# A hybrid decoder layer in float32: the gate product as seven block products for eight, and a DMA that adds to the output

## The chip, the cores and the metric

The kernel runs on one core of one Trainium2 chip. The metric is the device time of one execution in microseconds; before the change the median of three runs is 583.5 us (583.44 to 583.79).

## The reference

One decoder layer on 512 tokens of width 1024, in float32: an input projection, block-sparse attention beside a chunked spatial gating, an output projection, a channel MLP with squared ReLU (width 4096), and at the end a gated per-layer embedding. Only the end is changed:

```
h = h + rms_norm(jnp.einsum('bsf,fd->bsd', ff, w_down[i]), mlp_post_g[i])
gate = jax.nn.sigmoid(jnp.einsum('bsd,de->bse', h, w_ple_gate[i]) + b_ple_gate[i])
ple = jnp.einsum('bsp,pd->bsd', p[i], w_ple[i]) * gate
h = h + rms_norm(ple, ple_post_g[i])
```

rms_norm scales each token by one over the root of its mean square and multiplies by a gain row. The gate product is 512x1024 by 1024x1024.

## The kernel before, in words

**Products.** Float32 accuracy comes from splitting each operand into a high part that TensorE takes exactly (the copy to fp32r on ScalarE, "hi") and the remainder (a subtraction on VectorE, "lo"). `product` (line 2337) issues three matmuls for one pair of 128-row blocks: hi by hi, hi by lo, lo by hi. Tokens go in four tiles of 128 (t = 0 to 3), the 1024 output columns in two halves of W = 512. The MLP's up and down products already use a seven-product scheme (`up_product` 2702, `down_product` 2737); their right-hand sums are made partly by VectorE and partly by DMAs on GpSimd's queue that add to what lies in SBUF (`add_x`, line 2139).

**Order of work.** The order on each engine is written out by hand, and each engine goes through its list in order, waiting on semaphores. SyncE's list issues the loads and stores, GpSimd's the accumulating loads.

**The stage around the change.** After the last MLP products come eight tiles of the last part of the down projection (`down_tile`, 2770). For each VectorE adds PSUM to acc (`tail_down`, 1327); per token tile ScalarE squares (`square_down`, 1956), GpSimd takes the power (`rstd`, 2034; two small instructions), and VectorE scales acc and adds it to h (`add_mlp`, 1268; lines 1273 and 1278). TensorE turns h by transposes (`turn_h2`, 2798), ScalarE and VectorE take hi and lo of the turned h straight from PSUM (`h2_turn_lo`, 1281). Meanwhile the gate weights arrive in 8 pairs of 512-column slabs (`gate_pair`, 2251), are copied to hi (`gate_hi`, 1932) and split to lo (`split_lo`, 659, two instructions of 128x512 a pair).

**The gate tiles.** `gate_tile` (2803) makes the tiles of `GATE_TILES` (242), each (token tile, first column, width), nine in all, in the order of the tokens, the last half of token tile 3 in two tiles of 256 columns. A tile is 8 row blocks by three matmuls, 24. After it: VectorE adds the bias from PSUM to acc (`gate_bias`, 1287), ScalarE takes the sigmoid (1964; the last tile straight from PSUM, whose bank was seeded with the bias), VectorE multiplies by ple (`gate_ple`, 1298), ScalarE squares with a sum (`square_ple`, 1974), VectorE multiplies by the gain meanwhile (`gain_ple`, 1307). When the last tile of a token is squared, GpSimd adds the parts and takes the power (lines 2173 to 2194; for the very last tile the root of the sum of the other parts is taken first and squared in as an extra column), and VectorE scales by it and adds to h (`add_ple`, 1316), one instruction per tile. SyncE stores each piece as it is ready (2326).

## Time and profile before

| | |
|---|---|
| median of three runs | 583.5 us |
| span of the profiled execution (first to last instruction) | 581.5 us |
| mean granted TensorE clock, share of full speed | 0.996 |
| TensorE busy | 573.5 us, 99% |
| VectorE busy | 495.2 us, 85% |
| ScalarE busy | 356.4 us, 61% |
| GpSimd busy | 98.6 us, 17% |
| moved by DMA | 89.26 MB, mean 154 GB/s |

The table is read from the top: the profiled execution's own time is its span, 581.5 us, and the runs' median holds 2.0 us more than that span. The busy shares are averages over the whole; the stage that changes begins at about 503 us of the span and is looked at by itself below. In the rows PE is TensorE, PEld its weight load, DVE is VectorE, ACT is ScalarE, POOL is GpSimd and SP is SyncE. Busy times of neighbours can overlap: an instruction's duration is longer than the distance to the next start.

### The profile page before, as it was taken

To read this page: it belongs to the slowest core of one execution; us is meant where nothing else is said; L and a number is where in the kernel's file an instruction comes from. 1 tells how busy PE (TensorE), PEld (TensorE's weight loads), DVE (VectorE), ACT (ScalarE), POOL (GpSimd) and SP (SyncE) were. 2 spreads that over 40 slices of the span, in tenths; PEclk is the share of its full clock that TensorE was granted. 3 is DMA by queue.
4 is the path that set the end of the run, shared out by engine and by line. 5 is a ranking of instruction groups with operands and counts; after the bars stand their busy time and mean duration, and the time that the engine had idled before them with its cause. 6 is when DMAs were issued, how large, how long until landed. Compare 5 with 4: busy or idle time off the path is not lost.

```text
span 581.5 us, 8919 instructions
## 1 busy us (share of the span) xinstructions
PE 573.5 (99%) x3400; PEld 500.8 (86%) x3400; DVE 495.2 (85%) x639; ACT 356.4 (61%) x569; POOL 98.6 (17%) x152
## 2 busy tenths in 40 slices
PE   8999999999999999999999999999999999999995
PEld 7888888888888888989999999999989999988885
DVE  5899986688766998999989999999999899799664
ACT  6896675775646746667656665575655756654422
POOL 0331536000103463001010011010100100011011
PEclk9999999999999999999999999999999999999998
DMA  8982008223003559469485492774753936584011
GB/s 269 345 320 85 0 2 324 76 72 123 25 1 109 202 189 319 87 183 229 96 249 114 119 276 41 215 185 74 264 132 75 285 75 155 207 294 178 0 73 73
DMA packets 26250, 89.26 MB, mean 154 GB/s; under 512 B 3040, under 2 KB 4448, under 8 KB 25696
## 3 DMA queue, kind: packets, MB, share of 16 engines
q1 hardware_dynamic: 20448, 66.59, 32.6%
q0 software_dynamic: 4032, 14.68, 14.3%
q10 hardware_dynamic: 1728, 7.42, 3.4%
q8 instruction: 27, 0.44, 0.3%
q14 instruction: 15, 0.12, 0.1%
HBM read 82.40 MB, written 6.29 MB: 153 GB/s over the span
## 4 chain that ended last, share of the span: by engine, by line
PE 98%; DMA 1%; DVE 0%; ACT 0%; SPq 0%; issue 0%; POOL 0%; DVEq 0%; ACTq 0%
PE psum L2340 31%; PE psum L2344 30%; PE psum L2345 30%; PE psum L2395 2%; PE psum L2578 2%; PE psum L2558 2%; DMA first_raw_a<-weights_dram 1%; PE psum L2409 1%; PE psum L2432 0%; DVE h L1323 0%; ACT w_hi L1393 0%; POOL stat L2192 0%; PE psum L2463 0%; PE psum L2457 0%; PE psum L2437 0%
## 5 line engine op out<-in xcount | busy, mean ns | idle before, releaser
L2340 PE MATMUL psum<-t_hi,a_hi 128*128 128x512 f32 x216 | 84.8, 393 | 0.0
L2344 PE MATMUL psum<-t_lo,a_hi 128*128 128x512 f32 x216 | 84.6, 392 | 0.0
L2345 PE MATMUL psum<-t_hi,a_lo 128*128 128x512 f32 x216 | 84.0, 389 | 0.0
L2340 PE MATMUL psum<-w_hi,actT_hi 128*128 128x512 f32 (+1 forms) x190 | 73.6, 387 | 0.0
L2345 PE MATMUL psum<-w_hi,actT_lo 128*128 128x512 f32 (+1 forms) x190 | 72.4, 381 | 0.0
L2344 PE MATMUL psum<-w_lo,actT_hi 128*128 128x512 f32 (+1 forms) x190 | 72.3, 380 | 0.0
L2345 PE MATMUL psum<-sum_hi,up_lo 128*128 128x256 f32 x224 | 63.4, 283 | 0.0
L2344 PE MATMUL psum<-sum_lo,up_hi 128*128 128x256 f32 x224 | 63.4, 283 | 0.0
L2340 PE MATMUL psum<-sum_hi,up_hi 128*128 128x256 f32 x224 | 63.2, 282 | 0.0
L2345 PE MATMUL psum<-actT_hi,up_lo 128*128 128x256 f32 (+1 forms) x200 | 60.0, 300 | 0.0
L2344 PE MATMUL psum<-actT_lo,up_hi 128*128 128x256 f32 (+1 forms) x200 | 60.0, 300 | 0.0
L2340 PE MATMUL psum<-actT_hi,up_hi 128*128 128x256 f32 (+1 forms) x200 | 59.9, 299 | 0.0
L2142 POOL DMA_DIRECT2D raw_x<-weights_dram x21 | 18.6, 885 | 215.5 <-DVE t_lo L1130 215.1
L1189 DVE TENSOR_TENSOR acc<-acc,psum 128x512 f32<-128x512 f32 x76 | 49.0, 680 | 1.8 <-PE psum L2345 1.8
L985 DVE TENSOR_TENSOR up_lo<-raw,up_hi 128x1024 fp32r<-128x1024 f32 x37 | 46.7, 1262 | 2.6 <-ACT up_hi L1688 2.0
L2345 PEld LDWEIGHTS psum<-t_hi,a_lo 128*128 128x128 f32 x216 | 40.6, 188 | 8.9
L2340 PEld LDWEIGHTS psum<-t_hi,a_hi 128*128 128x128 f32 x216 | 40.7, 189 | 7.1
L2344 PEld LDWEIGHTS psum<-t_lo,a_hi 128*128 128x128 f32 x216 | 40.8, 189 | 6.6
L2344 PEld LDWEIGHTS psum<-sum_lo,up_hi 128*128 128x128 f32 x224 | 42.9, 191 | 1.1
L2340 PEld LDWEIGHTS psum<-sum_hi,up_hi 128*128 128x128 f32 x224 | 42.9, 191 | 1.1
L2345 PEld LDWEIGHTS psum<-sum_hi,up_lo 128*128 128x128 f32 x224 | 42.9, 191 | 0.0
L2345 PEld LDWEIGHTS psum<-w_hi,actT_lo 128*128 128x128 f32 x190 | 35.7, 188 | 6.9
(264 smaller groups left out, 1415.8 us busy)
## 6 DMA issues: line engine op xcount, KB each, us to landing
raw<-weights_dram SPq DMA_DIRECT2D x34, 512.0 KB, 4.5
raw_o<-weights_dram SPq DMA_DIRECT2D x23, 512.0 KB, 4.3
raw_x<-weights_dram POOLq DMA_DIRECT2D x21, 512.0 KB, 5.6
raw_second<-weights_dram SPq DMA_DIRECT2D x14, 512.0 KB, 4.2
raw_x<-weights_dram SPq DMA_DIRECT2D x9, 512.0 KB, 5.9
qk_raw<-weights_dram SPq DMA_DIRECT2D x8, 512.0 KB, 6.8
gate_raw<-weights_dram SPq DMA_DIRECT2D x8, 512.0 KB, 5.1
raw_o<-weights_dram POOLq DMA_DIRECT2D x7, 512.0 KB, 7.1
```

The lines of the kernel that those rows point to most:

```text
L985: nc.vector.tensor_tensor(up_lo[q % UP_SLOTS][:], block_source(step, j), up_hi[q % UP_SLOTS][:].bitcast(F32), ALU.subtract).then_inc(block ...
L1189: nc.vector.tensor_tensor(part, part, bank, how).then_inc(product_added, 1)
L2142: nc.gpsimd.dma_start(raw_x[step % 2][:], weights[down_in_stream(step, rows, half)], accum_op=ALU.add).then_inc(x_added, 16)
L2340: begin = nc.tensor.matmul(out, a_hi, b_hi, start=first, stop=False, skip_group_check=read_between)
L2344: nc.tensor.matmul(out, a_hi, b_lo, start=False, stop=False, skip_group_check=read_between)
L2345: return nc.tensor.matmul(out, a_lo, b_hi, start=False, stop=last, skip_group_check=read_between)
L2395: mm = nc.tensor.transpose(psum[:, banks[name], j * P:(j + 1) * P], source[:, j * P:(j + 1) * P], ident[:])
L2409: mm = nc.tensor.matmul(out, wsT[:, g, :], gv[:, :, g * GD:(g + 1) * GD], start=True, stop=True)
L2558: mm = nc.tensor.transpose(psum[:, bank + s, k * P:(k + 1) * P], probs[:, place_in_group(unit), s, k * P:(k + 1) * P], ident[:])
L2578: mm = nc.tensor.matmul(psum[s * DH:(s + 1) * DH, BANK_O, pair * P:(pair + 1) * P], v[:, k, head * DH:(head + 1) * DH], probsT_of[place_in ...
```

## The change

The gate product is made of seven block products. h has four blocks (token half by row half), the weights have four (row half by column half); the seven products use, on each side, blocks and sums of blocks. In the names below 11, 12, 21 and 22 are blocks, T1 to T4 sums of weight blocks and E, S2, S3 and S4 sums of blocks of h. Each product is made for the two token tiles of a half (j = 0, 1), 4 row blocks by three matmuls, 12 at 512 columns; the last is made in two parts of 256 columns. So there are 14 products, in the order of `GATE_PRODUCTS`.

- Weights: 14 halves of blocks, each 128x1024, are copied to hi by ScalarE and split by VectorE. T1 to T4 come from accumulating loads on GpSimd's queue: T1, T2 and T4 one after another onto the place of block 11, T3 onto a fresh load; each waits until the split of what lies there is done.
- h turned: ScalarE copies it from PSUM to SBUF (`h2_copy_raw`), copies the blocks that are used as they are to hi, and VectorE makes the sums E, S2, S3 and S4 for each j and their lo parts.
- Results: ScalarE seeds the PSUM banks with bias rows (the second is the sum of two, made by GpSimd in SBUF), copies three intermediate results to SBUF (`gate_copy`), and VectorE adds or subtracts (`gate_c11`, `gate_c22`, `gate_fold`). Half of the tiles' sigmoids read PSUM.
- Tiles now finish in the token order 2, 0, 3, 1. For tokens 2 and 0 SyncE stores h into the output early; VectorE then only scales (one scalar_tensor_tensor a tile with the gain row, no separate gain multiply, no add), and an accumulating DMA on GpSimd's queue adds 128x1024 to the output in DRAM.
- The gain row of the MLP, the bias row and the gain row of the embedding are loaded on SyncE's queue in places of their own; a load on ScalarE's queue goes.
- The loads `gate_x` (blocks 21, the base of T3, 22) wait for the split of what lay in their place before. On TensorE each product waits for its weight half, its activation and the bank (PSUM chain 0 and 1, side 2 and 3, E 4 and 5); among them (5, j) waits for `gate_c22(j)` and (6, j) for `gate_fold(j)`.

```diff
+GATE_11, GATE_21, GATE_T1, GATE_T2, GATE_T3, GATE_T4, GATE_22 = range(7)
+GATE_SPLITS = (GATE_11, GATE_T1, GATE_21, GATE_T2, GATE_T3, GATE_T4, GATE_22)
+GATE_SLOT = (1, 2, 0, 3, 1, 2, 0)
+GATE_PRODUCTS = ((0, 0), (1, 0), (0, 1), (1, 1), (2, 0), (3, 0), (2, 1), (4, 0), (3, 1), (5, 0), (4, 1), (6, 0),
+                 (5, 1), (6, 1))
+GATE_CHAIN, GATE_P1, GATE_E = 0, 2, 4
+H2_SPLIT = (0, 1, 2, 3, 5, 7)
+GATE_LAST_PART = GATE_P1 + 1
+OF_E, OF_S2, OF_S3, OF_S4 = range(4)
+GATE_SUMS_SPLIT = ((OF_E, 0), (OF_S2, 0), (OF_E, 1), (OF_S3, 0), (OF_S2, 1), (OF_S3, 1), (OF_S4, 0), (OF_S4, 1))
+GATE_SUMS = ((OF_E, 0), (OF_S2, 0), (OF_S3, 0), (OF_E, 1), (OF_S2, 1), (OF_S3, 1), (OF_S4, 0), (OF_S4, 1))
...
-GATE_TILES = ((0, 0, W), (1, 0, W), (0, W, W), (1, W, W), (2, 0, W), (2, W, W), (3, 0, W),
-              (3, W, W // 2), (3, W + W // 2, W // 2))
-SEEDED = len(GATE_TILES) - 1
+GATE_TILES = ((0, 0, W), (1, 0, W), (2, W, W), (2, 0, W), (3, W, W), (0, W, W), (3, 0, W),
+              (1, W, W // 2), (1, W + W // 2, W // 2))
+TOKENS_DONE = (2, 0, 3, 1)
+ADDED_IN_OUT = (2, 0)
+LAST_GATED = len(GATE_TILES) - 1
...
+            def h2_sum(which, j):
+                a11, a12, a21, a22 = h2_block(0, 0, j), h2_block(0, 1, j), h2_block(1, 0, j), h2_block(1, 1, j)
+                if which == OF_E:
+                    dve.wait_ge(h2_raw, 6 + 2 * j)
+                    first, second, how = a21, a22, ALU.subtract
+                elif which == OF_S2:
+                    dve.wait_ge(x_summed, gate_sum_at(OF_E, j))
+                    first, second, how = gate_e[:, j], a11, ALU.subtract
+                elif which == OF_S3:
+                    first, second, how = a11, a21, ALU.subtract
+                else:
+                    dve.wait_ge(x_summed, gate_sum_at(OF_S2, j))
+                    first, second, how = a12, gate_s2[:, j], ALU.add
+                nc.vector.tensor_tensor(gate_sum_source(which, j), first, second, how).then_inc(x_summed, 1)
...
+            def gate_c11(j):
+                dve.wait_ge(c_copied, gate_copy_at(COPY_C11, j))
+                dve.wait_ge(up_filled, gate_at(1, j))
+                part = acc[:, j, 0:W]
+                nc.vector.tensor_tensor(part, part, psum[:, GATE_P1 + j, :], ALU.add).then_inc(c_summed, 1)
...
+            def gate_fold(j):
+                dve.wait_ge(c_copied, gate_copy_at(COPY_CHAIN, j))
+                if j == 0:
+                    bank = psum[:, GATE_E, :]
+                    nc.vector.tensor_tensor(bank, bank, acc[:, 0, W:2 * W], ALU.subtract).then_inc(gate_folded, 1)
                     return
...
+                if t in ADDED_IN_OUT:
+                    if t == ADDED_IN_OUT[0]:
+                        dve.wait_ge(post_loaded, 48)
+                    dve.wait_ge(pl_rstd, TOKENS_DONE.index(t) + 1)
+                    for i in tiles:
+                        dve.wait_ge(pl_gated, i + 1)
+                        cut = slice(GATE_TILES[i][1], GATE_TILES[i][1] + GATE_TILES[i][2])
+                        nc.vector.scalar_tensor_tensor(out=ple_of(t)[:, cut], in0=acc[:, t, cut],
+                                                       scalar=rstd_pl[:, t:t + 1], in1=ple_gain[:, cut],
+                                                       op0=ALU.mult, op1=ALU.mult).then_inc(out_ready, 1)
+                    return
...
             tail_down(0)
             tail_down(1)
-            splits(SLAB_GATE + 6)
+            gate_split_lo(GATE_T1, 1)
             tail_down(2)
             add_mlp(0)
             tail_down(3)
-            splits(SLAB_GATE + KD)
+            gate_split_lo(GATE_21, 0)
             tail_down(4)
             tail_down(5)
             add_mlp(1)
-            h2_turn_lo(0)
-            h2_turn_lo(1)
-            splits(SLAB_GATE + KD + 2)
+            h2_split_lo(0)
+            h2_split_lo(1)
+            gate_split_lo(GATE_21, 1)
             tail_down(6)
             tail_down(7)
             add_mlp(2)
-            h2_turn_lo(2)
-            h2_turn_lo(3)
+            h2_split_lo(2)
+            h2_split_lo(3)
             add_mlp(3)
-            splits(SLAB_GATE + KD + 4)
-            h2_turn_lo(4)
-            h2_turn_lo(5)
-            splits(SLAB_GATE + KD + 6)
-            h2_turn_lo(6)
-            h2_turn_lo(7)
-            def seed_bias():
-                _, c0, width = GATE_TILES[SEEDED]
-                nc.vector.tensor_copy(psum[:, bank2["gate", SEEDED], 0:width], gate_rows[:, 0, c0:c0 + width]
-                                      ).then_inc(bias_seeded, 1)
-            for i, (t, c0, width) in enumerate(GATE_TILES):
-                gate_bias(i)
-                if i == SEEDED - 6:
-                    dve.wait_ge(*drained["gate", i])
-                    seed_bias()
-                gate_ple(i)
-                if i == gate_tiles_of(t)[-1]:
-                    add_ple(t, *gate_tiles_of(t))
-                else:
-                    gain_ple(i)
+            gate_split_lo(GATE_T2, 0)
+            gate_split_lo(GATE_T2, 1)
+            h2_sum(OF_E, 0)
+            h2_sum(OF_S2, 0)
+            h2_sum_split_lo(OF_E, 0)
+            h2_sum(OF_S3, 0)
+            h2_sum_split_lo(OF_S2, 0)
+            gate_c11(0)
+            gate_split_lo(GATE_T3, 0)
+            gate_split_lo(GATE_T3, 1)
+            h2_split_lo(5)
+            h2_sum(OF_E, 1)
+            h2_sum(OF_S2, 1)
+            h2_sum_split_lo(OF_E, 1)
+            h2_sum_split_lo(OF_S3, 0)
+            h2_sum_split_lo(OF_S2, 1)
+            h2_sum(OF_S3, 1)
+            gate_split_lo(GATE_T4, 0)
+            gate_split_lo(GATE_T4, 1)
+            gate_c11(1)
+            h2_sum(OF_S4, 0)
+            gate_fold(0)
+            gate_c22(0)
+            h2_sum_split_lo(OF_S3, 1)
+            h2_split_lo(7)
+            h2_sum(OF_S4, 1)
+            h2_sum_split_lo(OF_S4, 0)
+            gate_split_lo(GATE_22, 0)
+            gate_split_lo(GATE_22, 1)
+            gate_ple(0)
+            h2_sum_split_lo(OF_S4, 1)
+            gate_fold(1)
+            gate_ple(1)
+            gate_ple(2)
+            gate_ple(3)
+            gate_c22(1)
+            add_ple(2)
+            gain_ple(1)
+            gate_ple(4)
+            gain_ple(4)
+            gate_ple(5)
+            add_ple(0)
+            gate_ple(6)
+            add_ple(3)
+            gate_ple(7)
+            gain_ple(7)
+            gate_ple(8)
+            add_ple(1)
...
+            def h2_copy_raw(i):
+                t, k_half = divmod(i, 2)
+                if i == 0:
+                    act.wait_ge(a_lo_done, FIRST_LAST + 4)
+                act.wait_ge(filled, filled2["h2T", i])
+                nc.scalar.activation(h2_block(t // 2, k_half, t % 2), h2_turned(i), ACT.Copy).then_inc(h2_raw, 1)
+                drained["h2T", i] = (h2_raw, i + 1)
...
+                if (t < 2) == (c0 == 0):
+                    act.wait_ge(c_summed, gate_result_at(t // 2, j))
+                    nc.scalar.activation(z, z, ACT.Sigmoid).then_inc(sig_done, 1)
+                else:
+                    act.wait_ge(up_filled, gate_at(5 if c0 == 0 else 6, j) + (i == LAST_GATED))
+                    nc.scalar.activation(z, gate_result(i), ACT.Sigmoid).then_inc(sig_done, 1)
...
+            gate_split_hi(GATE_T1, 1)
             square_down(0)
-            gate_hi(4)
+            gate_split_hi(GATE_21, 0)
             square_down(1)
-            gate_hi(5)
-            h2_turn_hi(0)
-            h2_turn_hi(1)
+            gate_split_hi(GATE_21, 1)
+            seed_chain(0)
+            seed_chain(1)
+            for i in (0, 1):
+                h2_copy_raw(i)
+                h2_split_hi(i)
             square_down(2)
-            act.wait_ge(filled, filled2["down", 7])
-            act.dma_start(gate_rows[:], rows["gate"]).then_inc(gate_rows_loaded, 16)
-            h2_turn_hi(2)
-            h2_turn_hi(3)
+            for i in (2, 3):
+                h2_copy_raw(i)
+                h2_split_hi(i)
             square_down(3)
-            gate_hi(6)
-            h2_turn_hi(4)
-            h2_turn_hi(5)
-            gate_hi(7)
-            h2_turn_hi(6)
-            h2_turn_hi(7)
-            for i in range(len(GATE_TILES)):
+            gate_split_hi(GATE_T2, 0)
+            gate_split_hi(GATE_T2, 1)
+            seed_e(0)
+            seed_e(1)
+            gate_copy(COPY_C11, 0)
+            h2_copy_raw(4)
+            h2_copy_raw(5)
+            h2_split_hi(5)
+            h2_sum_split_hi(OF_E, 0)
+            h2_sum_split_hi(OF_S2, 0)
+            gate_copy(COPY_C11, 1)
+            gate_split_hi(GATE_T3, 0)
+            gate_split_hi(GATE_T3, 1)
+            h2_copy_raw(6)
+            h2_copy_raw(7)
+            h2_split_hi(7)
+            h2_sum_split_hi(OF_E, 1)
+            h2_sum_split_hi(OF_S3, 0)
+            h2_sum_split_hi(OF_S2, 1)
+            gate_copy(COPY_E, 0)
+            gate_copy(COPY_CHAIN, 0)
+            gate_split_hi(GATE_T4, 0)
+            gate_split_hi(GATE_T4, 1)
+            h2_sum_split_hi(OF_S3, 1)
+            gate_copy(COPY_E, 1)
+            sigmoid(0)
+            h2_sum_split_hi(OF_S4, 0)
+            gate_split_hi(GATE_22, 0)
+            gate_split_hi(GATE_22, 1)
+            h2_sum_split_hi(OF_S4, 1)
+            gate_copy(COPY_CHAIN, 1)
+            sigmoid(1)
+            square_ple(0)
+            sigmoid(2)
+            square_ple(1)
+            sigmoid(3)
+            square_ple(2)
+            square_ple(3)
+            for i in range(4, len(GATE_TILES)):
...
+            def add_gate(block, part):
+                pair = {GATE_T1: 4, GATE_T2: 6, GATE_T4: 2, GATE_T3: 6}[block] + part
+                if block == GATE_T3:
+                    pool.wait_ge(gate_x_loaded[part], first_load + 32)
+                else:
+                    before = {GATE_T1: GATE_11, GATE_T2: GATE_T1, GATE_T4: GATE_T2}[block]
+                    pool.wait_ge(block_lo, gate_split_at(before, part))
+                added = gate_x_added if block == GATE_T3 else gate_y_added[part]
+                nc.gpsimd.dma_start(gate_source(block, part), weights[gate_in_stream(pair)], accum_op=ALU.add
+                                    ).then_inc(added, 16)
...
+            add_gate(GATE_T1, 0)
+            add_gate(GATE_T1, 1)
+            pool.wait_ge(bias_loaded, 16)
+            nc.gpsimd.tensor_tensor(gate_bias_row[:, W:2 * W], gate_bias_row[:, 0:W], gate_bias_row[:, W:2 * W],
+                                    ALU.add).then_inc(bias_summed, 1)
+            add_gate(GATE_T2, 0)
+            down_rstd(0)
+            add_gate(GATE_T2, 1)
+            down_rstd(1)
+            down_rstd(2)
+            add_gate(GATE_T3, 0)
+            down_rstd(3)
+            add_gate(GATE_T3, 1)
+            add_gate(GATE_T4, 0)
+            add_gate(GATE_T4, 1)
...
+                if t in ADDED_IN_OUT:
+                    pool.wait_ge(stored, 16 * len(ADDED_IN_OUT))
+                    pool.wait_ge(out_ready, 2 * (n + 1))
+                    nc.gpsimd.dma_start(out[t * P:(t + 1) * P], ple_of(t), accum_op=ALU.add).then_inc(added_in_out, 16)
...
+            for t in ADDED_IN_OUT:
+                sp.wait_ge(h2_ready, t + 1)
+                sp.dma_start(out[t * P:(t + 1) * P], h[:, t, :]).then_inc(stored, 16)
...
+                for k in range(4):
+                    mm = product(out, x_high[:, k, :], x_low[:, k, :], w_high[:, k, columns], w_low[:, k, columns],
+                                 i == 1 and k == 0, k == 3, read_between=True)
+                mm.then_inc(up_filled, 1)
...
             down_tile(7)
             turn_h2(2)
             turn_h2(3)
-            gate_tile(0)
+            gate_product(0, 0)
+            gate_product(1, 0)
             turn_h2(4)
             turn_h2(5)
-            gate_tile(1)
+            gate_product(0, 1)
+            gate_product(1, 1)
             turn_h2(6)
             turn_h2(7)
-            for i in range(2, len(GATE_TILES)):
-                gate_tile(i)
+            for i, j in GATE_PRODUCTS[4:-1]:
+                gate_product(i, j)
+            gate_product(6, 1, 0)
+            gate_product(6, 1, 1)
```

## Rows read from the trace of the kernel before

**Rows 1.** The page: busy time (us, share, instructions); by engine, the chain that ended last.

```profile
PE 573.5 (99%) x3400; PEld 500.8 (86%) x3400; DVE 495.2 (85%) x639; ACT 356.4 (61%) x569; POOL 98.6 (17%) x152
...
PE 98%; DMA 1%; DVE 0%; ACT 0%; SPq 0%; issue 0%; POOL 0%; DVEq 0%; ACTq 0%
```

**Rows 2.** Timeline of PE in the gate stage: start us, duration us, engine, line, operation, tiles.

```profile
545.00 0.39 PE L2340 MATMUL psum<-w_hi,actT_hi 128*128 128x512 f32 x1
...
569.48 0.28 PE L2340 MATMUL psum<-w_hi,actT_hi 128*128 128x256 f32 x1
...
575.12 0.28 PE L2345 MATMUL psum<-w_hi,actT_lo 128*128 128x256 f32 x1
```

**Rows 3.** Timeline of DVE in the tail of the last tokens; in brackets idle before, releaser.

```profile
565.63 0.69 DVE L1305 TENSOR_TENSOR acc<-acc,ple_late_b 128x512 f32<-128x512 f32 x1 [0.70 <-ACT acc L1972]
...
568.20 1.41 DVE L1323 SCALAR_TENSOR_TENSOR h<-ple_late_b,stat,h 128x512 f32<-128x512 f32 x2 [1.16 <-POOL stat L2192]
...
577.48 1.54 DVE L1323 SCALAR_TENSOR_TENSOR h<-ple_late_b,stat,h 128x512 f32<-128x512 f32 x3 [0.74 <-POOL stat L2192]
```

**Rows 4.** Busy us by stretch: PE, PEld, DVE, ACT, POOL; PE clock, DMA share, GB/s.

```profile
508.00:536.00 28.00, 28.00 (x137) 23.42 (x137) 26.82 (x35) 13.97 (x26) 3.68 (x8) 1.00 0.68 253
536.00:562.00 26.00, 26.00 (x120) 21.57 (x119) 17.22 (x28) 10.25 (x21) 2.71 (x6) 1.00 0.11 41
562.00:579.00 17.00, 13.39 (x82) 11.90 (x80) 9.88 (x17) 5.23 (x14) 2.69 (x7) 0.95 0.08 32
```

**Rows 5.** Timeline of DVE where h2 is made and a weight pair split.

```profile
518.68 1.23 DVE L1278 TENSOR_TENSOR h<-h,acc 128x1024 f32<-128x1024 f32 x1
...
534.57 1.23 DVE L1278 TENSOR_TENSOR h<-h,acc 128x1024 f32<-128x1024 f32 x1
535.72 1.29 DVE L663 TENSOR_TENSOR w_lo<-gate_raw,w_hi 128x512 fp32r<-128x512 f32 x2
```

**Rows 6.** Source of the accumulating loads; landing of the plain output stores.

```profile
L2142 POOL DMA_DIRECT2D raw_x<-weights_dram x21: 875/875/1083, 221.4 to 480.3; - x21
...
DMA to landing us min/median/max: 5.2/5.6/10.6
...
DMA to landing us min/median/max: 2.0/2.0/2.1
```

**Rows 7.** Timeline of ACT: two copies of the down stage, the table load, squares.

```profile
506.85 1.05 ACT L1850 ACTIVATE t_hi<-raw_x 128x1024 fp32r<-128x1024 f32 x1
507.80 0.61 ACT L1861 ACTIVATE a_hi<-f 128x512 fp32r<-128x512 f32 x1
...
543.11 1.28 ACT L1972 ACT_TABLE_LOAD   x1
...
566.36 0.63 ACT L1427 ACTIVATE junk_late<-acc 128x512 f32<-128x512 f32 x1 [0.76 <-DVE acc L1305]
566.89 0.19 ACT L1427 ACTIVATION_READ_ACCUMULATOR junk_late<-acc 128x1 f32 x1
...
574.25 0.19 ACT L1427 ACTIVATION_READ_ACCUMULATOR junk_late<-acc 128x1 f32 x1
...
576.31 0.42 ACT L1427 ACTIVATE junk_late<-last_gated 128x257 f32<-128x257 f32 x1 [0.49 <-DVE last_gated L1305]
```

**Rows 8.** Timeline of POOL in the tail.

```profile
567.25 0.27 POOL L2190 TENSOR_SCALAR stat<-stat 128x1 f32<-128x1 f32 x1 [4.18 <-ACT junk_late L1427]
567.60 0.57 POOL L2192 TENSOR_TENSOR stat<-stat 128x1 f32<-128x1 f32 x1
...
575.28 0.57 POOL L2183 TENSOR_TENSOR last_gated<-stat 128x1 f32<-128x1 f32 x1
```

**Rows 9.** Tile xr: sums on POOL; timeline of DVE beside them.

```profile
L2125 POOL TENSOR_TENSOR actT_lo<-xr,actT_hi x4: 1273/1292/1747, 183.0 to 190.8; 128x512 fp32r<-128x512 f32 x4
...
L2152 POOL TENSOR_TENSOR xr<-xr x4: 2395/3257/3290, 208.7 to 217.8; 128x1024 f32<-128x1024 f32 x4
...
218.76 3.41 DVE L1102 TENSOR_TENSOR sum_lo<-xr,sum_hi 128x1024 fp32r<-128x1024 f32 x1
```

More of the change, by code:

```diff
@@ L223, in tail_results @@
             (("down", 5), 1), (("h2T", 0), 2), (("h2T", 1), 3), (("down", 6), 4), (("down", 7), 5),
[L224 to L227 removed]
+            (("h2T", 2), 6), (("h2T", 3), 7), (("h2T", 4), 6), (("h2T", 5), 7), (("h2T", 6), 6), (("h2T", 7), 7)]
     return [name for name, _ in late], dict(late)
@@ L1265, in _ @@
             add_product(FIRST_LAST - 1)
-            splits(SLAB_GATE + 4)
+            gate_split_lo(GATE_T1, 0)
             def add_mlp(t):
@@ L2327, in _ @@
                              ).then_inc(stored, 16)
-            sp.wait_ge(stored, 16 * len(order))
+            sp.wait_ge(added_in_out, 32 + 16 * len(ADDED_IN_OUT))
+            sp.wait_ge(stored, 16 * (len(ADDED_IN_OUT) + len(order) - 2 * len(ADDED_IN_OUT)))
         @block.tensor
```

338 lines of the change are left out of this document (232 added, 106 removed).

## The prediction

> **What bounds the kernel now.** I read the engine shares and the chain that ended last first [rows 1]: TensorE is busy 99% of the span and makes 98% of the chain, VectorE is busy 85%. Up to the last matmul this is a TensorE kernel. Then the stage that changes. From 545.00 to 569.48 TensorE starts 108 matmuls of 512 columns, one every 0.2267 us, and from there to 575.12 47 of 256, one every 0.12 us, without a gap; the last ends at 575.40 [rows 2]. What follows is a chain of small steps to the last VectorE instruction, which ends at 579.02 [rows 3], and the last store with the program's end takes the span to 581.5. Last, VectorE by stretches [rows 4]: 26.8 of 28 us from 508 to 536 (this includes overlaps of neighbours), then 17.2 of 26, then 9.9 of 17. So VectorE has no room before 536 and a third of its time after it; ScalarE has more. The question is whether the products that TensorE saves are paid for by work that fits into that room.
>
> **TensorE, removed.** The gate is 9 tiles: seven of 24 matmuls at 512 columns, two of 24 at 256. The new one is 13 products of 12 matmuls at 512 and two of 12 at 256. That is 168 - 156 = 12 fewer wide ones (2.72 us) and 24 fewer narrow ones (2.88 us): 5.60 us. With no new wait TensorE ends at 575.40 - 5.60 = 569.8. The transposes of h2 stay, and the granted clock is 1.00 in these stretches [rows 4].
>
> **VectorE, added.** Durations here are spacings, since neighbours overlap: 1.15 us for 128x1024 and 0.60 for 128x512 (two took 1.29 with the overlap) [rows 5], 0.67 for a scalar_tensor_tensor of 512 columns [rows 3]. Weight halves: 14 of 1024 columns (16.1 us) for 16 slabs of 512 (9.6): +6.5. Split remainders of activations: 6 of h2 and 8 of sums for 8: +3.6. New sums of h2: 8, +4.8. Results: 4 adds from PSUM and the folds (6 x 0.60 with one cut in two) for 8 bias adds and a seed: -1.2. The tiles of tokens 2 and 0 lose their gain multiplies, 4 x 0.60: -2.4. Together about +11 us, on an engine that behind 536 has some 16 us without work [rows 4], most of it in waits between the steps of a token's tail, and the change takes 5.6 us off the time itself.
>
> **Where the added work lies.** I followed each engine's new order with these spacings. Up to the fourth add_mlp little moves. The transposes wait for add_mlp(0), which ended at 519.9 [rows 5] with time in hand before the transposes of token 0; the splits before it are as long as the old ones. rstd(3) on GpSimd comes 0.5 us later, because ScalarE now makes four copies per h2 pair, not two, before square_down(3), and so add_mlp(3) ends not at 535.80 [rows 5] but at 536.3. The accumulating loads stand ahead of rstd(0) to rstd(3) in GpSimd's queue; each holds it for 0.88 us of issue [rows 6] and their waits are met earlier than the squares. They land 5.2 to 10.6 us after the issue [rows 6]; with the median 5.6 the first, issued at about 504.9 behind the first split, is in place at 510.6, and VectorE comes to its split at 512.4.
>
> From there to the end of gate_ple(3) VectorE's list is 8 halves (9.2 us), 26 instructions of 512 columns (15.6), the two small folds (0.7) and two dependent sums (0.2): 25.7 us, plus two waits for ScalarE that came out of following the two orders side by side (0.65 and 0.88 us): from 536.2 to 563.5. ScalarE itself has 8 halves at 0.95, 22 copies at 0.53, the table load and two sigmoids [rows 7], about 22 us, in the same 27. So gate_ple(3) starts at 562.9 and ends at 563.6. Its input, product (5,0), has been there since 558.5. Each product is met in time on this plan, the closest being (2,1), whose sum is ready 0.3 us before it, and (5,1), which waits 0.4 us for gate_c22(1). TensorE ends at 570.0 with a gain of 5.4 us, and VectorE is by then far behind.
>
> **The tail, where the time is lost.** For each token tile VectorE ends a round that it must go through in order: gate_ple, then ScalarE's square and its read-out (0.73 us), GpSimd's two steps with their hand-overs (1.1), then two adds (1.33). In the trace gate_ple starts at 565.63, the square at 566.36, GpSimd's pair runs from 567.25 to 568.17, the adds from 568.20 to 569.61 [rows 3, 7, 8]; without the gain between, which hides in the wait, a round is 3.9 us. In the kernel of before a round has 5.4 us of matmuls beside it. In the new one all four come after 562.9: tokens 2, 0, 3, 1.
> - Token 2: 562.87 + 3.91 = 566.78.
> - gain_ple(1), gate_ple(4), gain_ple(4): 1.92, to 568.70. Then gate_ple(5) waits 0.76 us: sigmoid(5) stands on ScalarE behind the square of tile 4.
> - Token 0: 569.46 + 3.91 = 573.37. Token 3: to 577.28.
> - Token 1: gate_ple(7) and gain_ple(7) 0.84, a wait of 0.5 for sigmoid(8), which stands behind the square of tile 7. gate_ple(8) starts at 578.6. The last square waits for GpSimd's root, which was ready 1.41 us after the square of tile 7 (574.44 to 575.85) [rows 7, 8], so it starts at 579.70. From there to the first add 1.17 us (576.31 to 577.48), and the three adds 1.54 [rows 3, 7]: VectorE ends at 582.41.
>
> **One price from elsewhere: the bias row.** GpSimd now adds two 512-column rows in SBUF at about 508, while VectorE is full. Such an instruction took 1.3 to 1.7 us on GpSimd, and a VectorE instruction beside GpSimd's sums took 3.41 us where one of its shape alone took 1.23 [rows 5, 9]. So I let VectorE stand still for 1.3 us there (bounds 0 and 2.2, the excess in those rows). A wait of 0.9 us for rstd(0) behind it swallows most of it, and 0.35 us reach the end.
> The Trainium skill (SBUF — State Buffer, section "SBUF: two separate sides") says that VectorE with two SBUF inputs and a GpSimd instruction that reads SBUF take turns on a shared port pair, the later one blocked for the whole of the other; by that rule it could also cost nothing where GpSimd is the one that waits. The trace agrees with the blocking [rows 5, 9].
>
> **The DMA that adds to the output.** h of tokens 2 and 0 is stored early (in the quiet DMA time behind 545) and GpSimd issues the adds after add_ple. The trace shows no such transfer into DRAM; the bounds are a plain store's 2.0 us and 10.6, the longest of the accumulating loads, and I take 5.6, the same size and kind [rows 6]. The last is issued at 573.9 and lands at 579.5, at worst at 584.5, ahead of the last store. The issue holds GpSimd until 574.8, when the square of tile 6 ends too: nothing. So it costs nothing at the end and its merit is the removed gain.
>
> **The sum.** VectorE's end 582.41 + 0.35 = 582.76, against 579.02: +3.7 us. Behind it stand the same three stores. Span 581.5 + 3.7 = 585.2; the profiled execution lies 2.0 us below the median of 583.5 (what lies around the span), so the forecast is 587.2 us.
>
> **The rivals.**
> 1. TensorE stays the bound (chance 0.06). Then everything ends 3.6 us after the last matmul, as now [rows 2, 3]: 569.8 + 3.6 = 573.4, 5.6 us less, 577.9. For it: TensorE is 98% of the chain, and no product waits for long. Against: four rounds of 3.9 us would have to lie in 11 us, on an engine that goes in order. This is the mechanism on the other side; it decides if rounds overlap or gate_ple(3) comes before about 554, which product (5,0) at 558.5 rules out.
> 2. The backlog is smaller than I count (0.12). With no backlog at all gate_ple(3) starts behind product (5,0), at 559.2 to 559.5, some 3.4 us sooner, and the tail of 19 us begins there: 587.2 - 3.4 = 583.8. This is a floor of the serial tail: even then no gain. A part of it gives 584 to 586.
> 3. The accumulating loads come late (0.14). Decides at a landing above some 7.6 us where they share the engines with the loads of h. Up to 2 us beyond the median waits swallow nearly all (+0.3). At 10.6 the first half reaches ScalarE 5 us later, VectorE's splits stand in line behind it, the add_mlp of token 0 holds the transposes and TensorE too, and later halves repeat it: by the same way of following, VectorE's end +5.9, 593.1. At 8.6: +1.9, 589.1.
> 4. The change is what it says in its count of matmuls; that it saves nothing on TensorE would need new gaps there (0.03, with the times of rival 3).
>
> **How the numbers follow.** The forecast as worked out has 0.65; its own range is 586.0 to 589.0: 0.02 us more or less on each of some 60 hand-overs and instructions moves the end by 0.5 to 1.8 us. The range for 8 in 10 goes down to 583.8, the floor of rival 2, and up to 590.5, the milder half of rival 3. A measurement of this kernel can tell about 0.2%, 1.2 us, from no change, so "same" is 582.3 to 584.7. Faster: rival 1 and a little of 2, 0.08. Same: the lower half of rival 2 and some error of mine, 0.12. Slower: 0.80.
>
> **What would show it.** Right: the last matmul ends at 569.5 to 571, VectorE's last instruction 11 to 14 us after it (3.6 now); VectorE over 90% busy from 536 to 562; in the last 19 us a pattern of waits on VectorE for GpSimd's rstd (over 1.1 us each, four times) and for sigmoids; gate_ple(3) at about 563; the chain's share of VectorE, ScalarE and GpSimd much above its present 1%. Wrong: a last VectorE instruction within 5 us of the last matmul (rival 1), gate_ple(3) before 560 (rival 2), ScalarE waiting over 3 us for an accumulating load (rival 3), or an end set by the DMA that adds to the output.

## The result and the profile after

The changed kernel takes 593.75 us (median of 4 runs, 593.14 to 594.22), the kernel before 583.64 on the same chip: ratio 1.0172, interval 1.0158 to 1.0187, so 10.1 us slower. Forecast were 587.2 and a range up to 590.5. The sign was right; the size is 6.5 us off and outside the range. The profiled execution has a span of 591.3 us.

The page: busy time by engine and the chain that ended last, to be held against [rows 1].

```profile
PE 571.2 (97%) x3364; PEld 497.8 (84%) x3364; DVE 507.4 (86%) x645; ACT 372.8 (63%) x591; POOL 108.5 (18%) x163
...
PE 91%; DVE 3%; DMA 2%; issue 2%; ACT 1%; POOL 1%; DVEq 0%; ACTq 0%; POOLq 0%
```

36 matmuls fewer, as the diff says. But TensorE's share of the chain falls from 98% to 91%, and DMA stands in it with 2% in place of 1%. One row of the chain makes the difference (start us, us, what it went through):

```profile
535.23 10.91 DMA raw<-weights_dram
```

The stretches, against [rows 4]:

```profile
508.00:536.00 28.00, 28.00 (x132) 22.72 (x131) 26.71 (x29) 18.20 (x30) 9.94 (x14) 1.00 0.83 210
536.00:562.00 26.00, 22.39 (x101) 18.26 (x99) 20.66 (x28) 17.31 (x27) 1.85 (x3) 0.93 0.79 214
562.00:579.00 17.00, 14.13 (x74) 11.91 (x72) 12.22 (x20) 8.36 (x20) 3.31 (x7) 1.00 0.19 33
```

The middle stretch is the surprise. TensorE stands idle for 3.6 of its 26 us, its clock is 0.93, VectorE is busy 20.7 us where it should have been full, and the DMA share went from 0.11 to 0.79. The timeline of ScalarE, then of GpSimd, then of SyncE's queue, shows why.

```profile
541.75 0.58 ACT L2204 ACTIVATE acc<-psum 128x512 f32<-128x512 f32 x1
546.16 2.01 ACT L2130 ACTIVATE w_hi<-raw 128x1024 fp32r<-128x1024 f32 x2 [3.83 <-DMA raw<-weights_dram]
```

```profile
530.57 0.91 POOL L2454 DMA_DIRECT2D raw<-weights_dram  x1 [0.30 <-POOL stat L2318]
...
535.23 0.90 POOL L2454 DMA_DIRECT2D raw<-weights_dram  x1 [0.30 <-POOL stat L2318]
```

```profile
529.99 0.43 SPq L2638 DMA_DIRECT2D ple_late_a<-ple_spill  x1
530.46 0.43 SPq L2639 DMA_DIRECT2D ple_gain<-row_gate_dram  x1
530.93 0.43 SPq L2640 DMA_DIRECT2D ple_late_b<-ple_spill  x1
```

The two accumulating loads of block T3 are issued at 530.57 and 535.23. In the same microsecond as the first, SyncE's queue sends off 2.5 MB for the tail (ple_late_a, ple_gain, ple_late_b), of which nothing is read before gate_ple(0) at 565.02. The second load of T3 lands at 546.1, 10.9 us after its issue. ScalarE waits 3.83 us for it, with both halves, as they share one semaphore and line L2130 asks for both. VectorE's splits of T3 wait behind ScalarE, and TensorE behind VectorE. Here is VectorE, then TensorE at that place:

```profile
547.26 2.36 DVE L1349 TENSOR_TENSOR w_lo<-raw,w_hi 128x1024 fp32r<-128x1024 f32 x2 [3.61 <-ACT w_hi L2130]
...
551.51 0.69 DVE L1405 TENSOR_TENSOR actT_lo<-gate_e,actT_hi 128x512 fp32r<-128x512 f32 x1
```

```profile
548.31 0.39 PE L2673 MATMUL psum<-w_hi,actT_lo 128*128 128x512 f32 x1
552.31 0.47 PE L2668 MATMUL psum<-w_hi,actT_hi 128*128 128x512 f32 x1 [3.61 <-issue]
...
553.19 0.63 PE L2668 MATMUL psum<-w_hi,actT_hi 128*128 128x512 f32 x1
553.62 0.63 PE L2672 MATMUL psum<-w_lo,actT_hi 128*128 128x512 f32 x1
...
575.85 0.28 PE L2673 MATMUL psum<-w_hi,actT_lo 128*128 128x256 f32 x1
```

The product that comes late is (2,1). It does not use T3 at all: it needs the low part of E(1), which VectorE ends at 552.20 because it stands in its list behind the two splits of T3. No run here puts it ahead of them.

Three matmuls start 0.30, 0.24 and 0.34 us apart behind the gap of 3.61 us, then 0.43 us apart in place of 0.227, until 556.2: half speed, the 1.2 GHz level. The granted clock from 552.3 to 556.2 is 0.58. The twelve starts from 552.31 on take 4.4 us where 2.7 would do, another 1.7 us. So TensorE's last matmul starts at 575.85, later than before the change (575.12, [rows 2]), though it has 5.6 us less to do. VectorE's tail begins that much later. Its timeline, against [rows 3]:

```profile
568.84 0.69 DVE L1443 TENSOR_TENSOR acc<-acc,ple_late_b 128x512 f32<-128x512 f32 x1 [0.67 <-ACT acc L2215]
...
578.24 1.41 DVE L1466 SCALAR_TENSOR_TENSOR ple_late_a<-acc,stat,ple_gain 128x512 f32<-128x512 f32 x2 [2.18 <-POOL stat L2496]
...
582.52 1.42 DVE L1475 SCALAR_TENSOR_TENSOR h<-ple_late_b,stat,h 128x512 f32<-128x512 f32 x2 [1.54 <-POOL stat L2496]
...
587.22 1.54 DVE L1475 SCALAR_TENSOR_TENSOR h<-ple_late_a,stat,h 128x512 f32<-128x512 f32 x3 [1.22 <-POOL stat L2496]
```

gate_ple(3) starts at 568.84 (forecast 562.9), and VectorE ends at 588.76, which is 19.9 us later (forecast 19.5). The tail is as foreseen; it starts 6 us late.

### The profile page after: what moved, and what is told of

The parts are those of the page before. It is cut to its first block, busy times and chain, and to the rows that moved or that the text cites. A ratio compares the mean times of both kernels' runs of the same rounds, so it can differ in the third digit from the quotient of the medians.

```text
span 591.3 us, 8923 instructions
## 1 busy us (share of the span) xinstructions
PE 571.2 (97%) x3364; PEld 497.8 (84%) x3364; DVE 507.4 (86%) x645; ACT 372.8 (63%) x591; POOL 108.5 (18%) x163
## 4 chain that ended last, share of the span: by engine, by line
PE 91%; DVE 3%; DMA 2%; issue 2%; ACT 1%; POOL 1%; DVEq 0%; ACTq 0%; POOLq 0%
PE psum L2668 28%; PE psum L2672 28%; PE psum L2673 28%; DMA raw<-weights_dram 2%; PE psum L2723 2%; PE psum L2906 2%; PE psum L2886 1%; ACT junk_late L1606 1%; PE psum L2777 1%; DVE acc L1443 1%; PE psum L2737 1%; DVE w_lo L1349 1%; DVE h L1475 0%; DVE actT_lo L1405 0%; PE psum L2760 0%
## 5 line engine op out<-in xcount | busy, mean ns | idle before, releaser
L2668 PE MATMUL psum<-w_hi,actT_hi 128*128 128x512 f32 (+1 forms) x178 | 70.5, 396 | 3.6 <-issue 3.6
L2673 PE MATMUL psum<-w_hi,actT_lo 128*128 128x512 f32 (+1 forms) x178 | 69.2, 389 | 0.0
L2672 PE MATMUL psum<-w_lo,actT_hi 128*128 128x512 f32 (+1 forms) x178 | 69.0, 388 | 0.0
L2668 PEld LDWEIGHTS psum<-w_hi,actT_hi 128*128 128x128 f32 x178 | 33.8, 190 | 10.7 <-issue 4.2
```

The costliest lines, as they stand in the source:

```text
L2668: begin = nc.tensor.matmul(out, a_hi, b_hi, start=first, stop=False, skip_group_check=read_between)
L2672: nc.tensor.matmul(out, a_hi, b_lo, start=False, stop=False, skip_group_check=read_between)
L2673: return nc.tensor.matmul(out, a_lo, b_hi, start=False, stop=last, skip_group_check=read_between)
```

## The experiments

Twelve kernels. Each time is a median beside runs of the kernel before on the same chip (583.4 to 583.6). The kernel before differs by up to 0.3 us from chip to chip, so where two experiments ran on different chips, the difference taken against the kernel before beside each is given too. In the expectations, which are set as quotes, e1 is experiment 1, e8 is 2, e6 is 3, e3 is 4, e4 is 5, e13 is 6, e2 is 7, e9 is 8, e10 is 9, and e11, e12 and e14 are 10, 11 and 12.

**1. The early loads moved.** SyncE's queue sends the three ple and gain loads behind the last weight block, at 545.96 in place of 529.99.

```
-  wait(down 7); load ple_late[0]; load ple_gain; load ple_late[1]
   gate_x(GATE_22, 0); gate_x(GATE_22, 1)
+  wait(down 7); load ple_late[0]; load ple_gain; load ple_late[1]
```

> The changed kernel with the three late loads on SyncE's queue (both halves of ple and the gain row, 2.5 MB in all) moved behind the two loads of weight block 22. Theory A (the last rounds of four tokens run one after another, and an accumulating load that shares the DMA engines with these loads adds a stall in the middle): the wait of 3.8 us of ScalarE for T3 goes, the stretch of TensorE at half clock goes, VectorE's end comes 4 to 6 us earlier, so 588 to 590 us, and the tail from gate_ple(3) on stays at 19 to 20 us. Rival B (the stall is all that is wrong, TensorE is the bound once it is gone): 578 to 580 us. Rival C (the accumulating load is slow by itself, or waits for GpSimd's queue): 593 to 594 us as before.

Measured: 588.07 us, ratio 1.0082 (1.0065 to 1.0099), 5.7 us below the changed kernel (5.4 against the kernel before beside each), in the range of theory A. ScalarE and VectorE in its timelines:

```profile
541.87 2.00 ACT L2130 ACTIVATE w_hi<-raw 128x1024 fp32r<-128x1024 f32 x2
```

```profile
563.60 0.69 DVE L1443 TENSOR_TENSOR acc<-acc,ple_late_b 128x512 f32<-128x512 f32 x1 [0.68 <-ACT acc L2215]
...
581.98 1.54 DVE L1475 SCALAR_TENSOR_TENSOR h<-ple_late_a,stat,h 128x512 f32<-128x512 f32 x3 [1.22 <-POOL stat L2496]
```

ScalarE comes to T3 at 541.87 and does not wait. TensorE has neither the gap nor the slow matmuls: 3.6 + 1.7 of the 5.7 us. The landings of the eight accumulating loads of the gate, in the changed kernel and then here:

```profile
DMA to landing us min/median/max: 5.2/8.6/11.0
```

```profile
DMA to landing us min/median/max: 5.2/5.7/7.9
```

gate_ple(3) comes at 563.60 and the tail is 19.9 us long. The time is 0.9 us above the forecast. The DMA share of the stretch from 536 to 562 is 0.83 here, no lower than the 0.79 of the changed kernel, so that share does not tell the two apart. What differs is the time of T3's loads, 530.0 to 546.2: a share of 0.98 with 280 GB/s in the changed kernel, 0.84 with 165 GB/s here. Whether T3's loads lose their time in the DMA engines or in the memory behind them no run separates.

**2. Was it the shared wait or the shared DMA engines?** In the changed kernel, with its loads as they are, the first half of T3 waits for its own load alone (the bias row is summed by a DMA as in 3, which frees a semaphore).

```
-  act.wait_ge(gate_x_added, 32)
+  act.wait_ge(*((bias_summed, 32), (gate_x_added, 16))[part])
```

> The changed kernel, its early loads left as they are, but ScalarE's first half of T3 waits for its own accumulating load alone (and the bias row is summed by a DMA, to free the semaphore, worth up to 0.6 us by itself). Theory A (it is the sharing of the DMA engines with 2.5 MB of early loads that makes T3 late, the shared wait is the smaller part): the second half's split still starts at about 545.5 to 546.5, the first half's 1 to 3 us before it, TensorE still stands idle 1.5 to 3.5 us there: 590.5 to 593.3 us. Rival B (the shared wait was the cause): the idle time of TensorE goes and the time is that of e1, 587.5 to 589 us.

Measured: 590.78 us, ratio 1.0133 (1.0116 to 1.015). ScalarE, then TensorE:

```profile
541.38 1.05 ACT L2130 ACTIVATE w_hi<-raw 128x1024 fp32r<-128x1024 f32 x1
545.62 1.06 ACT L2130 ACTIVATE w_hi<-raw 128x1024 fp32r<-128x1024 f32 x1 [3.19 <-DMA raw<-weights_dram]
```

```profile
550.63 0.47 PE L2668 MATMUL psum<-w_hi,actT_hi 128*128 128x512 f32 x1 [2.36 <-issue]
550.93 0.40 PE L2672 MATMUL psum<-w_lo,actT_hi 128*128 128x512 f32 x1
551.17 0.40 PE L2673 MATMUL psum<-w_hi,actT_lo 128*128 128x512 f32 x1
```

The first half goes at once, the second still waits until 545.62. TensorE's gap shrinks from 3.61 to 2.36 us, and behind the third the matmuls keep their spacing of 0.23 us. Of the 3.0 us won, 1.1 are the bias row's (experiment 3) and 1.9, by subtraction, the shared wait's with the slow matmuls that followed it; against experiment 3, on the same chip, it remains 3.8 us slower, through the late landing. So the load is the greater cause, the shared semaphore the lesser.

**3. The bias row.** On top of 1, GpSimd's addition of the two rows becomes an accumulating DMA.

```
-  gpsimd.tensor_tensor(row[:, W:2W], row[:, 0:W], row[:, W:2W], add)
+  gpsimd.dma_start(row[:, W:2W], rows["gate"][:, 0, 0:W], accum_op=add)
```

> e1_loads_late with the sum of the two bias rows made by an accumulating DMA in place of GpSimd's addition. Theory A (GpSimd's addition holds VectorE up through the port they share): in e1 the split beside it takes 3.05 us where its like takes 1.22, so with the addition gone it takes 1.2 to 1.3 and the tail additions of the h rows end 1.0 to 1.8 us earlier; of that 0.3 to 0.9 us reaches the end, since gate_ple(3) cannot start before about 563.1 (its product ends at 562.5): 587.2 to 587.8 us. Rival B (one more accumulating DMA in GpSimd's queue delays the others by as much): 588.1 to 589 us, and the landings of the accumulating loads grow by 1 us or more.

Measured: 586.95 us, ratio 1.0057 (1.004 to 1.0074), 1.1 us below experiment 1 (1.3 against the kernel before beside each), somewhat more than theory A's 0.3 to 0.9. The same split beside the addition in the changed kernel, with the addition on GpSimd, and then the split without it here:

```profile
508.05 3.05 DVE L1230 TENSOR_TENSOR t_lo<-raw_x,t_hi 128x1024 fp32r<-128x1024 f32 x1 [0.53 <-ACT t_hi L2029]
```

```profile
508.38 1.63 POOL L2464 TENSOR_TENSOR gate_bias_row<-gate_bias_row 128x512 f32<-128x512 f32 x1
```

```profile
507.81 1.22 DVE L1230 TENSOR_TENSOR t_lo<-raw_x,t_hi 128x1024 fp32r<-128x1024 f32 x1 [0.53 <-ACT t_hi L2029]
...
562.82 0.69 DVE L1443 TENSOR_TENSOR acc<-acc,ple_late_b 128x512 f32<-128x512 f32 x1 [0.67 <-ACT acc L2215]
```

The addition held VectorE up by 1.83 us. By the medians 1.1 of them reached the end, by the two profiled executions 0.8: gate_ple(3) starts at 562.82 here and at 563.60 in experiment 1. The wait for rstd(0) swallowed nothing, it is 0.48 us here and 0.47 there. VectorE comes to add_mlp(0) 1.5 us sooner here and loses part of this again, as it now stands 0.33 and 0.21 us for TensorE's tiles of the down projection.

**4. The output add, undone.** On top of 1, all four tokens are added to h on VectorE.

```
-ADDED_IN_OUT = (2, 0)
+ADDED_IN_OUT = ()
```

> e1 with the output add undone: tokens 2 and 0 end as in the kernel before (gain multiply, add to h, plain stores), no early store, no DMA that adds to DRAM. VectorE has four more multiplies of 0.6 us, most of them inside waits; GpSimd loses two issues of 0.9 us that stand before the powers of the next tokens. Theory A: within 0.8 us of e1, either way. Rival E (the adding DMA is what costs the time at the end): 2 us or more below e1. Rival F (the output add is a clear gain): 2 us or more above e1.

Measured: 588.22 us, ratio 1.0082 (1.0065 to 1.0099): no difference to 588.07. The multiplies that it saves lay in waits.

**5. The output add alone, in the kernel before** (tokens 0 and 1, which are the first there).

```
+  if t < 2: ple_of(t) = acc * rstd * gain (VectorE); GpSimd: DMA adds ple_of(t) onto out[t]
```

> The kernel before with the output add alone, for its first two token tiles 0 and 1: no gain multiply for their four tiles, the scaled part is added onto the stored h by DMA. Theory A: VectorE has idle time there and the last token sets the end, so 583.6 us within 0.5. Rival E (the adding DMA disturbs): above 585 us.

Measured: 583.85 us, ratio 1.0005 (0.9995 to 1.0014): no change. So the output add does not make the loss; it comes with the rest of the change.

**6. Less backlog ahead of the tail.** On top of 1, the eight low parts of the sums are made over one column in 128 only; the rest of them is left out.

```
-  tensor_tensor(lo, sum, hi, subtract)
+  tensor_tensor(lo[:, :, 0:1], sum[:, :, 0:1], hi[:, :, 0:1], subtract)
```

> e1_loads_late with the eight low parts of the sums made over one column in each 128 only, the rest left out: 8 times about 0.5 us of VectorE work gone ahead of gate_ple(3), nothing else. Theory A (the remaining loss of e1 is the serial tail; the backlog ahead of it is worth 1 to 2 us): gate_ple(3) starts at 561.8 to 562.6, held by its product and ScalarE, and the tail stays 19 to 20 us: 585.8 to 587.2 us. Rival B (the backlog is what costs, the tail shrinks with it): 583.5 to 585.5 us.

Measured: 586.52 us, ratio 1.0043 (1.0029 to 1.0058), 1.55 us below experiment 1 (1.8 against the kernel before beside each). VectorE:

```profile
536.86 1.23 DVE L1373 TENSOR_TENSOR h<-h,acc 128x1024 f32<-128x1024 f32 x1
...
562.64 0.69 DVE L1443 TENSOR_TENSOR acc<-acc,ple_late_b 128x512 f32<-128x512 f32 x1 [0.61 <-ACT acc L2215]
...
581.05 1.54 DVE L1475 SCALAR_TENSOR_TENSOR h<-ple_late_a,stat,h 128x512 f32<-128x512 f32 x3 [1.23 <-POOL stat L2496]
```

Some 4 us of work are gone, gate_ple(3) comes 0.96 us sooner, and the tail stays 19.95 us long, as theory A had it. This execution was already 0.86 us behind experiment 1 when add_mlp(3) ended (538.09 against 537.23), ahead of the first instruction that the edit touches, so the 4 us of work are worth 1.8 us at gate_ple(3). What is left is still 2.9 us above the kernel before: more than the backlog, it is the tail that costs.

**7. The tail in another order.** On top of 1, VectorE makes the next token's multiply before each final add, and GpSimd issues an output add behind the power of the next token.

```
-  gate_ple(3), gate_c22(1), add_ple(2), gain_ple(1), gate_ple(4), gain_ple(4), gate_ple(5), add_ple(0), gate_ple(6), ...
+  gate_ple(3), gate_c22(1), gain_ple(1), gate_ple(4), add_ple(2), gate_ple(5), gain_ple(4), gate_ple(6), add_ple(0), ...
```

> e1 with the same instructions in another order in the tail: on VectorE the gate_ple and gain_ple of the next tiles stand in the waits for GpSimd's power, and on GpSimd the issue of each output add stands behind the power of the next token. Theory A (the tail is bound by waits in a row): 4 to 6 us below e1, 583 to 585 us, TensorE's last matmul at the same time. Rival D (VectorE's amount of work is the bound from 537 to the end): within 1 us of e1. Rival B: no change from e1.

Measured: 585.7 us, ratio 1.0037 (1.0023 to 1.0051), 2.4 us below experiment 1, but less than theory A asked for. GpSimd, then ScalarE, at the end of the tail:

```profile
575.22 0.92 POOL L2504 DMA_DIRECT2D out_dram<-ple_late_a  x1 [0.30 <-POOL stat L2497]
575.87 1.36 POOL L2484 TENSOR_SCALAR stat<-stat 128x1 f32<-128x1 f32 x2
577.31 0.57 POOL L2488 TENSOR_TENSOR last_gated<-stat 128x1 f32<-128x1 f32 x1
```

```profile
577.96 0.42 ACT L1607 ACTIVATE junk_late<-last_gated 128x257 f32<-128x257 f32 x1 [3.12 <-POOL last_gated L2488]
```

GpSimd is now the slow link. The issue and two steps stand before the root, for which the last square waits 3.12 us; with VectorE busy beside them GpSimd's powers take 0.76 to 1.12 us instead of 0.57.

**8. The sigmoids ahead of the squares,** on top of 7.

```
-  sigmoid(2), square_ple(1), sigmoid(3), ..., sigmoid(8), square_ple(8)
+  sigmoid(1), sigmoid(2), square_ple(0), sigmoid(3), ..., square_ple(2), sigmoid(4), sigmoid(5), square_ple(3), ...
```

> e2_tail with ScalarE's sigmoids of the last tiles ahead of the squares of the earlier ones, so that no sigmoid whose product is ready waits behind a square that waits for VectorE. Theory A (the rounds of the tail are a chain through ScalarE and VectorE, and each sigmoid stands 1 to 3 us behind its product): gate_ple(3) starts at 563.3 to 563.5 instead of 564.0, the last sigmoid at about 571.5 instead of 574.5, the last VectorE instruction ends 1 to 3 us earlier, held by GpSimd's steps: 582.7 to 584.7 us. Rival B (GpSimd's small steps and its two DMA issues set the end alone): within 0.6 us of e2, 585.1 to 586.3 us.

Measured: 585.49 us, ratio 1.0035 (1.0024 to 1.0047). Theory A fell. gate_ple(3) came 0.8 us and the last sigmoid 2.2 us sooner, but VectorE then waited 1.77 us for GpSimd's first power, and the root, which starts at 577.55 (577.31 in 7), held the last square for 3.23 us. GpSimd sets the end, as rival B had it.

**9. GpSimd reduced to one power per token,** on top of 1 and the sigmoids of 8: the sums of squares are put together by VectorE with 0.13 us each, the root of the last token is not taken ahead, and VectorE's multiplies stand in its waits.

```
+  vector.tensor_scalar(mean, ss[b], ss[a], EPS, add, add)
-  gpsimd: two additions, then the power
+  gpsimd: the power
```

> e1_loads_late with the sigmoids ahead as in e9, the sums of squares put together by VectorE's tiny additions so that GpSimd has only one power per token, and VectorE's gains and multiplies filled into the waits. Theory A (the loss of the change is in the serial tail, and no engine's work there is too much: VectorE has about 12.5 us of it from gate_ple(3) on at 563.3): VectorE ends at 575.9 to 577.5, span 579 to 581, time 580.8 to 583.0 us, below the 583.4 us of the kernel before. Rival B (VectorE's backlog ahead of gate_ple(3) or GpSimd's power keeps a round of 2 us or more): 583.5 to 585.5 us.

Measured: 583.77 us, ratio 1.0003 (0.9994 to 1.0013): level with the kernel before, 4.3 us below experiment 1, and in the range of rival B. VectorE has one long wait left, for a power that stands behind the issue of an output add. VectorE, then GpSimd:

```profile
570.85 1.41 DVE L1482 SCALAR_TENSOR_TENSOR ple_late_a<-acc,stat,ple_gain 128x512 f32<-128x512 f32 x2 [1.41 <-POOL stat L2507]
```

```profile
569.33 0.90 POOL L2513 DMA_DIRECT2D out_dram<-ple_late_b  x1 [2.12 <-DVE ple_late_b L1482]
569.95 0.86 POOL L2507 TENSOR_TENSOR stat<-stat 128x1 f32<-128x1 f32 x1
```

**10 to 12. The parts joined.** All three have the tail of 9 and the bias row of 3. The first issues each output add behind the next token's power, the second has no output adds, the third keeps the one of token 2.

> e10_short_tail with the bias row summed by a DMA as in e6, and GpSimd's issue of each output add put behind the power of the next token. In e10 VectorE stood 1.41 us for a power that stood behind such an issue, and everything ahead of gate_ple(3) was VectorE's backlog. Theory A (both are on the path): gate_ple(3) 0.5 to 0.9 us earlier, the wait of 1.41 us down to under 0.5, VectorE ends at 575.5 to 576.8 instead of 577.7: 581.5 to 582.6 us, below the kernel before. Rival B (the end is then set by the second output add, issued later, that lands 5.3 us after its issue): 583 to 584 us.

> e10_short_tail with the bias row summed by a DMA and without the output adds: all four tokens are added to h on VectorE, four gains of 0.60 us more. Theory A (with the waits of the tail filled, VectorE's work itself is the path, so what the output add saves now counts, while it was hidden in e3): part of 2.4 us, less what GpSimd gains by issuing no DMA: 0.3 to 2 us above e11. Rival B (the output adds cost as much through GpSimd's issues as they save): equal to e11 within 0.3 us, or below it.

> e11_joined with the output add kept for token tile 2 alone; token tile 0 goes to h on VectorE again, its two gains of 0.60 us put where VectorE waited (0.83 and 0.44 us). Theory A (in e11 the end was the landing of the second output add, issued at 573.7 and 5.5 us on its way, and in e12 VectorE's own last addition at 577.65): the first output add is issued by about 570.5 and lands by 576.5, VectorE ends at 576.6 to 577.4, which is 0.3 to 1 us ahead of e12: 581.7 to 582.5 us. Rival B (any issue by GpSimd costs the powers behind it as much as two gains): within 0.3 us of e12, or above it.

```
   both: power(2), power(0), issue(2), power(3), issue(0), power(1)
   none: ADDED_IN_OUT = (); one: ADDED_IN_OUT = (2,)
```

Measured: with both output adds 583.35 us, ratio 0.9996 (0.9988 to 1.0005); with none 582.75, ratio 0.9983 (0.9974 to 0.9991); with one 582.34, ratio 0.9984 (0.9975 to 0.9993; the kernel before at 583.36 beside it, at 583.63 beside the other two). The last two are below both kernels, by 0.2% against the one before. The last additions of VectorE and the landing of the last two stores, with both output adds and then with none:

```profile
575.64 1.54 DVE L1490 SCALAR_TENSOR_TENSOR h<-ple_late_a,stat,h 128x512 f32<-128x512 f32 x3 [0.43 <-POOL stat L2507]
```

```profile
out_dram<-h SPq DMA_DIRECT2D x2, 128.0 KB, 3.9
```

```profile
576.11 1.54 DVE L1490 SCALAR_TENSOR_TENSOR h<-ple_late_a,stat,h 128x512 f32<-128x512 f32 x3
```

```profile
out_dram<-h SPq DMA_DIRECT2D x2, 128.0 KB, 2.5
```

With both adds VectorE ends 0.5 us sooner (577.18 against 577.65), but the span of the profiled execution is 1.2 us longer (582.2 against 581.0; the medians differ by 0.6): the accumulating stores are under way when the last stores leave, which then land after 3.9 us, not 2.5 (3.0 with one output add). Theory A of the first kernel fell, and theory A of the second (the saved multiplies count) too. The first kernel's time is in the range of its rival B, but not by the landing that this rival named, since 573.7 + 5.5 is 579.2 and not the end. With one add VectorE ends at 577.71, no sooner than with none, where a power beside the filled-in multiply took 1.46 us; by the ratios one add and none are the same, rival B of the third.

## Why the prediction was wrong, point by point

- **TensorE, -5.6 us: right as a count, wrong in "each product is met in time" (forecast end 570.0).** It held once the loads were moved: the last matmul ended at 570.9 in experiment 1 and at 570.1 in experiment 3. In the changed kernel itself it was 575.85, and the product that stood was (2,1), the one the prediction named as the closest.
- **The step that failed** is the timing of the accumulating loads. I took 5.6 us for all of them, the median of 21 loads between 221 and 485 us, where the DMA engines were busy 0.63 of the time at 165 GB/s, and of rival 3 I followed only T1's halves. The loads in danger were T3's, which took 10.9 us: the change issues 2.5 MB on SyncE's queue beside the first of them and ahead of the second, which made a share of 0.98 at 280 GB/s while they were on their way. The bytes and their order were to be had from the kernels. The prediction also nowhere counts that both halves of T3 wait on one semaphore, and rival 3 does not follow what stands behind T3 in VectorE's list, E(1) for product (2,1). This step is 5.4 to 5.7 us (experiment 1) of the 6.5 that were missing. The sign of failure that rival 3 named, ScalarE over 3 us in a wait for an accumulating load, is what the profile shows, at another block. Rival 3's end of 593.1 was near the result by luck, as it was worked out for T1's halves.
- **The bias row, +0.35: mis-sized.** The mechanism was right: VectorE stood for 1.83 us (priced 1.3). But 0.8 to 1.3 us reached the end: the wait for rstd(0) of 0.9 us that was to swallow most of it measured 0.47 us and was 0.48 without the addition, so it swallowed nothing. That and the first step make 6.3 to 6.5 of the 6.5 us. The Trainium skill (SBUF — State Buffer, section "SBUF: two separate sides") has the later of the two instructions blocked for the whole of the other on the shared port pair; the trace agrees in the size of the delay, 1.83 us beside a GpSimd instruction of 1.63 us, but not in the order: by the profile VectorE's instruction starts first (508.05 against 508.38), and yet it is the one held up.
- **VectorE's backlog: right.** gate_ple(3) at 562.82 in experiment 3, without late loads and bias row, against 562.87; at 563.60 in experiment 1.
- **The serial tail: right.** Forecast 19.5 us from gate_ple(3) to VectorE's end, measured 19.9 in three kernels (changed, experiments 1 and 6), with the waits for GpSimd where they were foreseen (2.18, 1.54 and 1.22 us for three of the four tokens). In the first round VectorE stands 1.34 us; the profile names no releaser, but GpSimd's power ends at 571.38 and VectorE goes on at 571.47.
- **The output add costs nothing and gains nothing: right** for the changed kernel with its loads moved and for the one before (experiments 4 and 5), and it landed 5.3 us after its issue (taken: 5.6). The time behind 545 was not quiet, as the prediction had it (a DMA share of 0.67 from 545 to 562), and this cost nothing. The output add stops being free once the tail is short.
- **Rival 1** (TensorE stays the bound) fell. **Rival 2** (backlog): with 4 us of VectorE's work gone 1.6 to 1.8 us came back; the rest went into VectorE's waits for ScalarE, 0.35 to 1.15 us each, and the floor of 583.8 was not reached. That the tail is to blame and not VectorE's total work shows in experiment 9, where another order and steps moved from GpSimd to VectorE bring back 4.3 us, with none of VectorE's work taken away.

Against the kernel before, the 10.1 us are then, each experiment taken against the kernel before beside it, 5.4 us of late loads with what TensorE's clock added, 1.3 us of the bias row and, by subtraction, 3.4 us of a tail in which four rounds come one after another and of the backlog ahead of it. The last is what the 5.6 us saved on TensorE could not pay for.

## What to carry to other kernels

When a change moves loads, add up the bytes in flight at each issue by queue and time, and price every later transfer that an engine waits for at the loaded duration, not at the median of another stage; check too which of them share a semaphore, and what else stands behind them in the lists of the engines that wait. When the bound engine is relieved, the serial chain of small steps behind it becomes the end: fill it (multiplies into the waits, sigmoids before squares, the fewest steps on the slowest engine) before the saving can be seen. Here the two best arrangements kept 0.9 to 1.0 us of the 5.6 saved.

## What the runs showed of the hardware

- Among the gate's accumulating loads of 512 KB the quickest took 5.2 us; the two of T3 took 10.9 (median) when issued beside, and 4.3 us behind, 2.5 MB of plain loads, and 5.7 without these.
- After 3.61 us without a matmul TensorE made three starts 0.24 to 0.34 us apart and then ran 0.43 us per 512 columns for some 3 us (the 1.2 GHz level; granted clock 0.58 from 552.3 to 556.2); after 2.36 us without one (experiment 2) it began at 0.30 and 0.24 and kept 0.23.
- In the tail GpSimd's one-column power took 0.55 to 0.58 us while VectorE stood and 0.76 to 1.46 beside a busy VectorE. So GpSimd slows down in just the tail that one fills up.
- The last plain stores of 128 KB landed after 2.5 us without accumulating stores, 3.0 with one and 3.9 with two of them shortly ahead (experiments 10 to 12), and after 2.1 us in the changed kernel, where the stores leave later behind them.
